# Five modulation blocks summed over their row chunks by VectorE in a two-layer hybrid trunk

## The reference, cut to what matters

```python
mod = (jax.nn.silu(cond) @ mod_w[l] + mod_b[l])[:, None, :]
sh1, sc1, g1, sh2, sc2, g2 = jnp.split(mod, 6, axis=-1)
h = _rms(x, norm_g[l, 0]) * (1.0 + sc1) + sh1
```

## Time and profile before

| | |
|---|---|
| median of 3 runs | 855.13 us (855.04 to 855.77) |
| profiled execution | 854.18 us |
| its span | 851.9 us |
| mean granted TensorE clock | 0.993 |
| weights and inputs read | 290.10 MB |

### The profile page before, as it was taken

How to read it: one execution, slowest core, us unless ns; L and a number is a source line. 1 busy time by engine, 2 the same in 40 slices (tenths; PEclk the granted TensorE clock), 3 DMA queues, 4 the chain that set the end, 5 groups by cost and what they waited for, 6 DMA issues and landing times.

```text
span 851.9 us, 13351 instructions
## 1 busy us (share of the span) xinstructions
PE 817.5 (96%) x5760; PEld 510.6 (60%) x5760; DVE 284.2 (33%) x587; ACT 176.3 (21%) x308; POOL 38.0 (4%) x67
## 2 busy tenths in 40 slices
PE   4999999899899999999999999999899999999997
PEld 3777778787643555445446888788644554455534
DVE  2246533614631111212124844571631112121213
ACT  4165013411501110111013212300411101110111
POOL 3200100030300000000000000000120000000000
PEclk9999999899999999999999999999999999999999
DMA  9999866785699999999999969357589999999991
GB/s 343 372 335 371 300 224 236 281 281 208 261 399 425 421 425 426 424 422 425 424 414 386 360 240 335 117 209 285 195 325 421 425 424 422 425 422 425 427 417 63
DMA packets 69221, 292.54 MB, mean 343 GB/s; under 512 B 4017, under 2 KB 6182, under 8 KB 48628
## 3 DMA queue, kind: packets, MB, share of 16 engines
q1 hardware_dynamic: 67156, 289.70, 86.2%
q10 hardware_dynamic: 1248, 1.08, 0.5%
q0 software_dynamic: 768, 1.04, 0.4%
HBM read 290.10 MB, written 1.70 MB: 343 GB/s over the span
## 4 chain that ended last, share of the span: by engine, by line
PE 86%; DVE 7%; DMA 4%; ACT 2%; issue 1%; SPq 0%; DVEq 0%
PE ps L1955 25%; PE ps L1983 12%; PE ps L2093 7%; PE ps L1931 6%; PE ps L1535 4%; PE ps L1998 4%; PE ps L1599 4%; PE ps L1721 3%; PE ps L1807 3%; PE ps L1593 3%; PE ps L1574 3%; DMA ring<-in_moe_w_up 3%; PE ps L2089 1%; DVE xT L1205 1%; PE ps L1708 1%
## 5 line engine op out<-in xcount | busy, mean ns | idle before, releaser
L1955 PE MATMUL ps<-ring,arena 128*64 128x512 f32 x832 | 223.4, 593 | 3.2 <-ACT arena L848 1.7
L1955 PEld LDWEIGHTS ps<-ring,arena 128*64 128x64 f32 x832 | 72.2, 137 | 110.8 <-issue 107.7
L1983 PE MATMUL ps<-ring,arena 128*64 128x512 f32 x512 | 113.4, 595 | 1.1 <-ACT arena L856 1.1
L1983 PEld LDWEIGHTS ps<-ring,arena 128*64 128x64 f32 x512 | 36.2, 137 | 66.4 <-issue 63.1
L1326 DVE SCALAR_TENSOR_TENSOR arena<-ps,arena 128x256 f32<-128x256 f32 x32 | 20.0, 667 | 152.8 <-PE ps L1955 152.8
L2093 PE MATMUL ps<-hs,ring 128*128 128x256 f32 x320 | 70.3, 380 | 0.0
L2093 PEld LDWEIGHTS ps<-hs,ring 128*128 128x128 f32 x320 | 60.5, 190 | 9.3 <-issue 1.4
L1931 PE MATMUL ps<-arena 128*128 (+1 forms) x512 | 60.0, 275 | 0.0
L1931 PEld LDWEIGHTS ps<-arena 128*128 128x128 f32 x512 | 58.4, 192 | 0.4 <-issue 0.4
L1955 PE MATMUL ps<-hs,arena 128*64 128x512 f32 x128 | 56.3, 593 | 0.0
L1535 PE MATMUL ps<-ring,csil 128*32 128x128 f32 x1536 | 50.8, 290 | 2.1 <-DVE arena L967 2.1
(11 more groups left out here) (312 smaller groups left out, 873.3 us busy)
## 6 DMA issues: line engine op xcount, KB each, us to landing
ring<-in_moe_w_up SPq DMA_DIRECT2D x64, 1024.0 KB, 16.3
ring<-in_moe_w_down SPq DMA_DIRECT2D x64, 1024.0 KB, 13.3
ring<-in_mod_w SPq DMA_DIRECT2D x24, 2048.0 KB, 13.2
ring<-in_moe_w_gate SPq DMA_DIRECT2D x20, 2048.0 KB, 13.3
hs<-in_moe_w_gate SPq DMA_DIRECT2D x8, 2048.0 KB, 15.5
ring<-in_hy_in_w SPq DMA_DIRECT2D x6, 2048.0 KB, 14.3
ring<-in_ab_in_w SPq DMA_DIRECT2D x4, 2048.0 KB, 12.8
arena<-in_moe_w_gate SPq DMA_DIRECT2D x4, 2048.0 KB, 15.2
```

What stands on the lines that cost most here:

```text
L1955: ins = mm(bank(4 + w)[e * 64:e * 64 + 64, :], xg[:, k, e * 64:e * 64 + 64], weights[:, k, :], start=(k == 0), stop=(k == KD - 1))
L1983: ins = mm(bank(6 + half)[e * 64:e * 64 + 64, :], hidT[:, f, e * 64:e * 64 + 64], down_unit(n + 4 + e)[:, f, half * 512:half * 512 + 512], ...
```

## The change

Blocks 5, 6 and 7 of layer 0 and 18 and 19 (layer 1) are no longer made by `mod_row`. For each of them VectorE sums the 8 chunks first: `fold(m, ks)` multiplies chunk k of the weights, 128 by 512, with the conditioning of its partition and adds it to an accumulator, once for each of the two rows of conditioning (one accumulator is free scratch, the other the unit's first chunk itself). `folded_row(m)` on TensorE then only sums over partitions: two accumulators by four groups of 128 columns, against a constant matrix `pick` that holds ones in column 0 or 1. The chunks are spread over VectorE's program: block 5 in three parts ahead of the QK norm, after it and after the products with q, block 6 whole ahead of the predicated copies, block 7 in three parts around the states; blocks 18 and 19 as 16 chunks over columns 5 to 15. The takes of these blocks move behind. On TensorE block 5 moves from part (4, 0) to (6, 0), 6 from (5, 0) to (6, 1), 7 from (6, 0) to behind the latent scores, and into bank 7; 18 from column 6 to column 12; 19 stays after column 16. Block 8 is taken before 7. GpSimd fills `pick` at the start. To free a semaphore, `m_half` becomes the first of five counts of `m_add` for each layer.

```diff
-        if _j >= 3 and _c < 2:
-            SCHED += [("RS"[_c], _j + 1)]
-SCHED += [("R", 8), ("U", 1, 1), ("sc", 1), ("S", 8), ("R", 9), ("ex1",), ...
+        SCHED += {(3, 0): [("R", 4)], (6, 0): [("F", 5)], (6, 1): [("F", 6)]}.get((_j, _c), [])
+SCHED += [("R", 8), ("U", 1, 1), ("sc", 1), ("F", 7), ("S", 8), ("R", 9), ("ex1",), ...
+FOLDED = [5, 6, 7, 18, 19]
+TURNS = sorted(MOD_AT, key=MOD_AT.get)
+TURNS[TURNS.index(7):TURNS.index(7) + 2] = [8, 7]
+        pick = sb("pick", [P, NS, 32])
+            link(pool, "g_chain", nc.gpsimd.memset(pick[:], 0.0))
+            for s in range(NS):
+                nc.gpsimd.memset(pick[:, s, s:s + 1], 1.0)
...
-                    act.wait_ge(q["m_half"], l + 1)
+                    act.wait_ge(q["m_add"], 5 * l + 1)
...
+            def fold(m, ks):
+                w = unit(MOD_AT[m])
+                if 0 in ks:
+                    dve.wait_ge(q["a_cs"], 1)
+                    arrived(dve, MOD_AT[m])
+                for k in ks:
+                    for s, acc in enumerate([fold_scratch(m), w[:, 0, :]]):
+                        c = csil[:, k, s:s + 1]
+                        if k == 0:
+                            ins = v.tensor_scalar(acc, w[:, 0, :], c, None, ALU.mult)
+                        else:
+                            ins = v.scalar_tensor_tensor(out=acc, in0=w[:, k, :], scalar=c, in1=acc, op0=ALU.mult, op1=ALU.add)
+                    if k == KD - 1:
+                        ins.then_inc(q["d_fold"], 1)
+                    else:
+                        L(ins)
...
             take_mod(4)
+            fold(5, range(0, 3))
...
-            take_mod(5)
+            fold(5, range(3, 6))
...
-            take_mod(6)
+            fold(5, range(6, 8))
+            fold(6, range(8))
...
-            take_mod(7)
+            take_mod(5)
+            fold(7, range(0, 3))
+            take_mod(6)
...
+                if d == 0:
+                    fold(7, range(3, 5))
...
+                if d == 0:
+                    fold(7, range(5, 8))
...
             score_max(1, 0, 4, 256, 48)
+            take_mod(7)
...
-                if j in (4, 7, 16):
-                    take_mod({4: 17, 7: 18, 16: 19}[j])
+                if j in (4, 13, 16):
+                    take_mod({4: 17, 13: 18, 16: 19}[j])
+                if 5 <= j <= 15:
+                    done = [0, 1, 4, 5, 6, 8, 9, 11, 12, 14, 15, 16]
+                    for c in range(done[j - 5], done[j - 4]):
+                        fold(18 + c // KD, (c % KD,))
...
+            def folded_row(m):
+                n = MOD_AT[m]
+                pe.wait_ge(q["d_fold"], FOLDED.index(m) + 1)
+                pe.wait_ge(q["g_const"], 8)
+                if m != 7:
+                    pe.wait_ge(q["d_mod"], MOD_TURN[m])
+                ...
+                for s, acc in enumerate(accs):
+                    for g in range(4):
+                        ins = mm(mod_bank(m)[32 * g:32 * g + 32, 0:128], pick[:, s, :],
+                                 acc.rearrange("p (b g c) -> p b g c", b=4, g=4)[:, :, g, :], start=(s == 0), stop=(s == 1))
+                used(ins, n)
...
             def squares(half):
                 pe.wait_ge(q["a_osq"], half + 1)
+                pe.wait_ge(q["d_mod"], MOD_TURN[7] + 1)
...
-                if j in (3, 6):
-                    mod_row(17 + (j == 6))
+                if j == 3:
+                    mod_row(17)
+                if j == 12:
+                    folded_row(18)
...
-                        mod_row(19)
+                        folded_row(19)
```

More of the change, by code:

```diff
@@ L65 @@
         SCHED += [("proj", _j, _c)] + _GAPS.get((_j, _c), [])
-        if _j >= 3 and _c < 2:
-            SCHED += [("RS"[_c], _j + 1)]
-SCHED += [("R", 8), ("U", 1, 1), ("sc", 1), ("S", 8), ("R", 9), ("ex1",), ("S", 9), ("o",), ("oss", 0), ("sc", 0),
+        SCHED += {(3, 0): [("R", 4)], (6, 0): [("F", 5)], (6, 1): [("F", 6)]}.get((_j, _c), [])
+SCHED += [("R", 8), ("U", 1, 1), ("sc", 1), ("F", 7), ("S", 8), ("R", 9), ("ex1",), ("S", 9), ("o",), ("oss", 0), ("sc", 0),
           ("pT", 1), ("oss", 1), ("ex0",), ("pv", 1), ("R", 12), ("pT", 0), ("S", 12), ("R", 13), ("oT", 1), ("S", 13),
@@ L183 @@
 H0_ACT = [(2, 3), (6, 7)]
-MOD_TURN = {m: i for i, m in enumerate(sorted(MOD_AT, key=MOD_AT.get))}
+FOLDED = [5, 6, 7, 18, 19]
+TURNS = sorted(MOD_AT, key=MOD_AT.get)
+TURNS[TURNS.index(7):TURNS.index(7) + 2] = [8, 7]
+MOD_TURN = {m: i for i, m in enumerate(TURNS)}
 LAST_MODS = [(10, 11), (22, 23)]
@@ L369, in build @@
             t_log a_htm d_lg a_re d_mask t_pos t_ST d_ST t_htm
-            m_add m_half m_xg a_xg d_xg a_sg d_hid m_hT a_hT d_hT a_y d_y
+            m_add m_xg a_xg d_xg a_sg d_hid m_hT a_hT d_hT a_y d_y
             d_flag d_scl0 up_low_in up_low_free down_low_in down_low_free hy_l hy_a hy_r hy_s hy_f hy_fd hy_k a_k t_u a_u d_uc d_zz t_zt a_zt a_zd t_spec a_spec
-            d_spec t_y d_r t_fin a_fin d_fin d_chain a_chain g_chain""".split()
+            d_spec t_y d_r t_fin a_fin d_fin d_chain a_chain g_chain d_fold""".split()
         q = {n: sem(n) for n in names}
@@ L391, in mod_bank @@
         def mod_bank(m):
-            return bank({1: 4, 2: 5, 3: 5}.get(m, 3 if 16 <= m <= 20 else 6))
+            return bank({7: 7, 1: 4, 2: 5, 3: 5}.get(m, 3 if 16 <= m <= 20 else 6))
         def unit(n):
@@ L971, in take_mod, with fold_scratch @@
                 L(v.tensor_tensor(modT[:, l, j:j + 4], mrow(m).rearrange("p (b c) -> p b c", b=4)[:, :, 0:NS], bias, ALU.add))
+            def fold_scratch(m):
+                return {5: A["S1"][:, 1024:1536], 6: A["S1"][:, 1536:2048], 7: X[0][:, 0:512],
+                        18: t1[:, 0:512], 19: t1[:, 512:1024]}[m]
+            def fold(m, ks):
[14 more added lines that the diff above has]
+                        L(ins)
             def scales(n):
@@ L1196, in residual @@
                     if units is None:
-                        dve.wait_ge(q["m_add"], 4 * l + b + 1)
+                        dve.wait_ge(q["m_add"], 5 * l + b + 2)
                     elif b % 2 == 0:
@@ L1529, in mod_row @@
                 elif m > 2:
-                    pe.wait_ge(q["d_mod"], MOD_TURN[m] - (m == 3))
+                    pe.wait_ge(q["d_mod"], MOD_TURN[m] - (m in (3, 9)))
                 if m in (14, 15):
@@ L1537, in mod_row @@
                                  start=(k == 0), stop=(k == KD - 1))
+                used(ins, n)
[5 more added lines that the diff above has]
+                    pe.wait_ge(q["d_mod"], MOD_TURN[m])
+                accs = [{5: A["S1"][:, 1024:1536], 6: A["S1"][:, 1536:2048], 7: X[0][:, 0:512],
+                         18: t1[:, 0:512], 19: t1[:, 512:1024]}[m], unit(n)[:, 0, :]]
+                for s, acc in enumerate(accs):
+                    for g in range(4):
+                        ins = mm(mod_bank(m)[32 * g:32 * g + 32, 0:128], pick[:, s, :],
+                                 acc.rearrange("p (b g c) -> p b g c", b=4, g=4)[:, :, g, :], start=(s == 0), stop=(s == 1))
                 used(ins, n)
@@ L1759, in _ @@
                     mod_row(*a)
+                elif what == "F":
+                    folded_row(*a)
                 elif what == "at":
@@ L1988, in down @@
                             if last and 2 in fs and half == 0:
-                                ins.then_inc(q["m_half"], 1)
+                                ins.then_inc(q["m_add"], 1)
                         if 0 in fs:
```

## The result

The changed kernel takes 863.32 us (median of 6, 861.21 to 866.16) where the kernel before took 855.25 beside it: ratio 1.0094, 95% interval 1.0075 to 1.0113. The forecast was 857.9, the range ended at 860.4. The profiled execution of the changed kernel takes 862.68 us, its span is 860.3: 8.4 more than the span of before.

A forecast was written before the change was run, and what follows sets the result against it. TensorE was taken to bound the kernel (busy 96%, 86% of the chain), VectorE's work being free only if in time. Front -1.2, block 19 +2.3, clock +1.7 gave +2.8 us on 855.13: 857.9 us, range 852.8 to 860.4.

The forecast's parts named there:

- the sum: Total of front -1.2, block 19 +2.3 and clock +1.7: +2.8 us, median 857.9 us; the forecast itself had chance 0.38.
- Removed from TensorE: Passes saved by folding: 1.41 us a block, 4.23 in first stretch, 2.82 in Hyena, 7.05 if VectorE is never late.
- At nothing: Effects priced at zero: GpSimd's pick memsets, the squares' wait, take order, m_half into m_add, later ring slots.
- three signs of being wrong: A pair under 1.38 us, a wait ahead of block 19 under 3 us, or a clock staying at 1.00 behind it.
- Front: Layer 0's first stretch: blocks 5, 6, 7 folded, less waits at two chunk states, move the recurrence's end by -1.2 us.
- the first pair of a block: VectorE's two tensor_scalar for a block's first chunk: one column a cycle, 0.68 us each, 1.31 the pair.
- The row at 413 ns: Profile row of tensor_scalar with a scalar per partition at 256 columns, used against two columns a cycle.
- Block 19: Hyena input projection: TensorE waits 5.3 us for VectorE's chunks; the block ends at 528.5 instead of 526.18, +2.3 us.
- The clock: Granted clock falls during TensorE's wait for block 19, costing between nothing and +3.4 us; middle taken, +1.7.
- Rival 4: The half-clock stretch at 160 goes away as the work ahead shifts: -3.4 + 2.8, 854.5 us; chance 0.06.
- Rivals 1 and 2: 1: VectorE late, clock stays up, +1.1, 856.2 us, chance 0.25; 2: VectorE keeps up, around 853, chance 0.19.
- Rival 3: More is late: pairs near 1.5 us, clock also falling in first stretch, or 3.4 us lost: 859.6 to 861; chance 0.12.

The follow-up runs named there:

- g3: Changed kernel with 24 unread products of a constant at the start; only the Hyena entry was read (idle time there), no total time given.
- e2: Changed kernel with only blocks 18 and 19 folded, 5, 6 and 7 by mod_row as before: 860.35 us, ratio 1.0062.
- f1: Changed kernel with 8 unread products ahead of layer 0's first norm, each to another quarter of the bank: 858.08 us, ratio 1.0022.
- f3: Changed kernel with the 8 unread products, plus 16 products of zeros filling TensorE's wait ahead of block 19: 855.95 us, ratio 0.9988.
- e1: Changed kernel with only blocks 5, 6 and 7 folded, 18 and 19 by mod_row as before: 860.17 us, ratio 1.0063.
- h3: Kernel before with 4 unread products ahead of the first norm; only the Hyena entry was read (no idle time there), no total time given.
- f4: Kernel before with 56 unread products at the start, each to another quarter of the bank: 860.28 us, ratio 1.004.
- h1: Kernel before with 64 unread products, 48 at the start and 16 ahead of the first norm: 854.4 us, ratio 0.9981.
- e4: Kernel before with 56 unread products at the start, all to one part of a bank: 869.51 us.

## Why the prediction was wrong

**The step that failed is the sum, which had no term for TensorE's code.** "Removed from TensorE" counted a product's time and nothing else, and "At nothing" doesn't list its code. None of the three signs of being wrong that the prediction names came: a pair took 1.45 us, the wait ahead of block 19 4.55, and the clock fell. But a product is also code, and 72 fewer move all code behind them. The whole program has 120 products less, and the page's queue of instructions shows it in packets of 16 KB (packets, MB, share): 39 before, and after

```profile
q8 instruction: 37, 0.61, 0.3%
```

38 in kernels with 48 to 88 products less, 40 with 56 or 64 more. A packet is thus about 60 products, and 64 if a product is four instructions (two weight loads, two passes, as the page counts) of 64 bytes. The Trainium skill (Trainium Architecture — The Big Picture, The software stack) has 64-byte instructions; the packets agree. In the kernel before a packet lands in the us from 451, 6 us ahead of the first column; after the change none lands on this queue between 434 and 456, among weights that hold the DMA engines at 1.03 of their time, and the next lands in the us from 456, when TensorE already stands. This queue's line in the windows 451:452 of before and 456:457 of after:

```profile
q8 instruction: 1, 0.02, 6.9%
```

```profile
q8 instruction: 1, 0.02, 6.8%
```

The other traces agree: in the six others with idle time a packet lands in the us after the one in which TensorE stopped, in the nine others without it one lands 4 to 7 us ahead of the first column. (In g3 one came 7 us ahead of the stop too, and didn't help.) I read it so: in most places the code behind the jump over the fallback is fetched only when TensorE gets there. That the place decides is shown by the seventeen kernels; how the fetch chooses its moment is not. The price, 4.3 us, is what puts 863.3 outside a range that ended at 860.4: without it the ratio was 1.0022, and the forecast's 857.9 by 855.13 is 1.0032.

**Front, -1.2 forecast, -2.05 measured.** The mechanism was right, VectorE late at both states, for 1.02 and 1.19 us instead of 1.7 and 1.3. The mis-sized term is the first pair of a block: 480 ns an instruction, not 680; with it the pair takes 0.91 us, not 1.31. The shorter waits are 0.8 of the 0.85 us. The Trainium skill (VectorE: DVE Perf Modes, The perf-mode tier table) has two elements a cycle for it, and the measurement sides with the page: 480 ns at 512 columns against 746 for the other form. The row at 413 ns for 256 columns, by which I chose, was a bad neighbour: a line through it and the row at 694 for 1024 gives 507 ns at 512, close to what was measured. A folded block took 0.64 us where 0.47 was forecast.

**Block 19, +2.3 forecast, +2.4 measured.** The wait was 4.55 us instead of 5.3, of which the first pair explains 0.4.

**The clock, +1.7 forecast, +2.2 in this trace** (1.5 and 1.7 in e2 and f1). It was right, and the filled wait shows the cause. The Trainium skill (TensorE: Matmul & The Clock Gate, HAM oscillation — how this bites in real kernels) has idle gaps bring the half rate; f1 and f3 agree. Not foreseen was that the same happens at the entry (e1 from 456.5, not in the trace of the change).

**Rival 4** had 3.4 us for the low stretch at 160. It did go away: in the change's trace the clock held from 160 to 167, but was at half from 150.4 to 153.8 instead. What such a stretch costs shows between the squares behind the recurrence and the experts' first products: 82.19 us in the kernel before (150.37 to 232.56), 82.54 after the change, and 81.05 in e2, where the clock held. That is 1.1 us for the stretch at 160, as TensorE at full clock waits 2.00 us for VectorE ahead of block 13 instead. So it is not worth its length, and it comes and goes: of the kernels with the front of before, h3 has it (82.19), f4 and h1 don't (81.05).

Rivals 1 and 2 were wrong by their conditions (the clock fell, VectorE was late). Rival 3, at 859.6 to 861, came nearest, but what made the time was none of its causes.

## What to carry to other kernels

Taking instructions off an engine moves its later code, and where a loop or a skipped block ends that can cost more than the work saved: look for "issue" in front of the first instruction behind a jump, and try a few products more or less ahead of it before judging a change of half a per cent. Give another engine only the pieces that it can finish before they are asked for: blocks 5, 6 and 18 gained, 19 cost 2.4 us of waiting and 2 us of clock. A wait of 4.5 us that stayed was 2 us cheaper filled with useless products than left empty.

## What was not expected of the hardware

The kernel before owes 0.4 to 0.6% to the place of its code (1.004 against 1, or against 0.9981): with 56 useless products at its start, in time in which TensorE waits anyway, it takes 860.28 us for 856.00, and with 64 it takes 854.4. Only the products can make the latter gain, but how is not shown. Behind 48 products the first 16 transposes took 1.97 us instead of 3.67, at a granted clock that the profile gives as 1.00 both times; yet in its trace the kernel with 64 comes to the experts 2.0 us earlier than before (230.52 for 232.56) and to their last scatter 0.2 later (453.77 for 453.58), after 3.3 us of waiting for weights there instead of 1.6. And the same 96 passes took 13.1 us into one quarter of a bank (e4) and 5.1 into four in turn (f4).
